# Silu out of the bank on ScalarE, and the norm weight in the product with the gates

## What is computed

```python
def _layer(x, ...):
    proj = x @ w_in                                  # hq hf hi hg rq rk rv rg su
    k_hg, log_f = ...                                # from sigmoid(hf)
    o_hg, s_hg = _chunked_gated_linear(silu(hq), k_hg, hi, log_f, s_hg)
    o_hg = o_hg * rsqrt(mean(o_hg ** 2) + EPS)
    o_hg = o_hg * hg_norm_w * silu(hg)
    o_rt, s_rt = _chunked_gated_linear(rotary(rq), rotary(rk), rv, log_gamma, s_rt)
    o_rt = (o_rt - mean) * rsqrt(var + EPS) * ret_norm_w
    o_rt = o_rt * silu(rg)
    y5 = gelu(s5_scan(su)); y5 = y5 * sigmoid(y5 @ glu_w + glu_b)
    x = layer_norm(ALPHA * x + concat(o_hg, o_rt, y5) @ w_out)
    return layer_norm(ALPHA * x + relu(x @ w_up) ** 2 @ w_down)
```

## Time and profile before

| | us |
|---|---|
| median of 3 runs | 898.17 |
| the profiled execution | 898.88 |
| its span | 897.1 |
| TensorE busy in matmuls | 780.9 |
| VectorE busy | 566.1 |
| ScalarE busy | 381.1 |
| GpSimd busy | 34.9 |

### The profile page before, as it was taken

The page is one execution under the profiler, slowest core; times in us unless marked ns, Lnnn a source line. Parts: engine busy times, 40 slices in busy tenths (PEclk is TensorE's granted clock), DMA queues, the critical chain, the costliest instruction groups (busy, mean ns, idle before and its releaser), DMA issues. The chain is left out here.

```text
span 897.1 us, 16462 instructions
## 1 busy us (share of the span) xinstructions
PE 780.9 (87%) x6750; PEld 736.6 (82%) x6750; DVE 566.1 (63%) x984; ACT 381.1 (42%) x668; POOL 34.9 (4%) x43
## 2 busy tenths in 40 slices
PE   3779778998979978999997987978897999999994
PEld 3778667788879877999996886777796999999993
DVE  7896895334466699764445787745456665466543
ACT  4453111443365622456336622424435554355433
POOL 4000010210000000000000000102000000000000
PEclk9898886987979999999996998989897999999998
DMA  8442111261425534654651332323151566555631
GB/s 333 127 129 72 48 48 48 79 215 45 144 71 165 164 116 143 189 175 129 183 172 48 95 96 71 110 72 102 48 164 38 175 172 195 179 184 169 189 114 49
DMA packets 30587, 113.58 MB, mean 127 GB/s; under 512 B 3520, under 2 KB 3712, under 8 KB 30000
## 3 DMA queue, kind: packets, MB, share of 16 engines
q1 hardware_dynamic: 27936, 101.83, 37.6%
q0 software_dynamic: 2000, 9.62, 2.9%
q10 hardware_dynamic: 576, 1.08, 0.3%
HBM read 108.33 MB, written 4.18 MB: 125 GB/s over the span
## 5 line engine op out<-in xcount | busy, mean ns | idle before, releaser
L1286 DVE TENSOR_TENSOR w_low<-w_raw,w_high 128x1024 fp32r<-128x1024 f32 x192 | 236.9, 1234 | 210.1 <-ACT w_high L949 208.0
L904 PE MATMUL stream<-a_high,w_high 128*128 128x264 f32 x1024 | 319.9, 312 | 43.2 <-DVE a_low L1291 30.2
L949 ACT ACTIVATE w_high<-w_raw 128x1024 fp32r<-128x1024 f32 x192 | 202.1, 1053 | 291.9 <-PE stream L906 257.0
L905 PE MATMUL stream<-a_low,w_high 128*128 128x264 f32 x1024 | 307.5, 300 | 0.0
L906 PE MATMUL stream<-a_high,w_low 128*128 128x264 f32 x1024 | 306.2, 299 | 0.0
L904 PEld LDWEIGHTS stream<-a_high,w_high 128*128 128x128 f32 x1024 | 210.1, 205 | 56.9 <-issue 22.4
L905 PEld LDWEIGHTS stream<-a_low,w_high 128*128 128x128 f32 x1024 | 211.3, 206 | 0.5
L906 PEld LDWEIGHTS stream<-a_high,w_low 128*128 128x128 f32 x1024 | 209.6, 205 | 0.0
L904 PE MATMUL stream<-h_high,w_high 128*128 128x264 f32 x512 | 149.2, 291 | 11.9 <-DVE w_low L1286 9.8
L905 PE MATMUL stream<-h_low,w_high 128*128 128x264 f32 x512 | 145.2, 284 | 0.0
L906 PE MATMUL stream<-h_high,w_low 128*128 128x264 f32 x512 | 145.1, 283 | 0.0
(11 more groups left out here) (325 smaller groups left out, 770.2 us busy)
## 6 DMA issues: line engine op xcount, KB each, us to landing
w_raw<-in_weights SPq DMA_DIRECT2D x192, 512.0 KB, 3.6
mats<-in_matrices POOLq DMA_DIRECT2D x2, 1024.0 KB, 5.4
S_hg<-in_state_hg POOLq DMA_DIRECT2D x2, 768.0 KB, 6.6
out_hg_s<-S_hg POOLq DMA_DIRECT2D x2, 768.0 KB, 4.5
consts<-in_constants POOLq DMA_DIRECT2D x1, 1484.5 KB, 9.4
X<-in_xT ACTq DMA_DIRECT2D x4, 264.0 KB, 5.9
out_y<-X SPq DMA_DIRECT2D x1, 1056.0 KB, 4.0
S_rt<-in_state_rt POOLq DMA_DIRECT2D x2, 512.0 KB, 8.1
```

The lines of the kernel that those rows point to most:

```text
L904: pe.matmul(bnk[:, 0:T], wh, xh, start=(first and kk == 0), stop=False)
L905: pe.matmul(bnk[:, 0:T], wh, xl, start=False, stop=False)
L949: act.activation(w_high[:, n % SPLIT_SLOTS, :], w_raw[:, n % RAW_SLOTS, :], ACT.Copy).then_inc(high_ready, 1)
L1286: put(tt(w_low[:, n % SPLIT_SLOTS, :], w_raw[:, n % RAW_SLOTS, :], w_high[:, n % SPLIT_SLOTS, :].bitcast(F32), ALU.subtract), low_ready)
```

## The change

Silu takes the place of Sigmoid for the queries and the gates, out of the same bank, and ScalarE frees these banks. VectorE's two kinds of products with the banks go. The wide products of `MIX` with the gates become three each, with the norm weight of the feature as a column scale.

```diff
@@ -291,7 +291,6 @@
         y5_done, y5_free = sem("y5_done"), sem("y5_free")
         u_ready = sem("u_ready")
         sig_ready = sem("sig_ready")
-        qsig_ready = sem("qsig_ready")
         gsig_ready = sem("gsig_ready")
         v_ready = sem("v_ready")
         rqk_ready = sem("rqk_ready")
@@ -635,7 +634,7 @@
                     return
                 if r == 0:
                     pe.wait_ge(first_ready, 2 * l + 1)
-                    pe.wait_ge(q_ready, l + 1)
+                    pe.wait_ge(q_ready, 3 * l + 3)
                 pe.wait_ge(dec_ready, 9 * l + r + 1)
                 banks = [unit(l, ("hg_level", r, p)) for p in range(3)]
 
@@ -991,8 +990,9 @@
                     copied(near_top_ready, 9 * l + done, fu)
 
             def gate_sigmoid(l, i):
-                p, _ = tile(l, HGT + i)
-                act.activation(gates[:, i, :], p, ACT.Sigmoid).then_inc(gsig_ready, 1)
+                p, fr = tile(l, HGT + i)
+                act.activation(gates[:, i, :], p, ACT.Silu).then_inc(gsig_ready, 1)
+                copied(gsig_ready, 6 * l + i + 1, fr)
 
             def mixer_work(l, c):
 
@@ -1011,7 +1011,8 @@
                 elif HQ < c <= HQ + 3:
                     i = c - 1 - HQ
                     p, fr = tile(l, HQ + i)
-                    act.activation(Qg[:, i, :], p, ACT.Sigmoid).then_inc(qsig_ready, 1)
+                    act.activation(Qg[:, i, :], p, ACT.Silu).then_inc(q_ready, 1)
+                    copied(q_ready, 3 * l + i + 1, fr)
                 elif SU < c <= SU + 2:
                     i = c - 1 - SU
                     p, fr = tile(l, SU + i)
@@ -1437,12 +1438,6 @@
                 put(tt(s5_end[:, 0, js, :], p1[:, 0, :, :], p3[:, 1, :, :], ALU.subtract))
                 put(tt(s5_end[:, 1, js, :], p1[:, 1, :, :], p3[:, 0, :, :], ALU.add), s5end_ready)
 
-            def hgrn_q(l, j):
-                dve.wait_ge(qsig_ready, 3 * l + j + 1)
-                p, fr = tile(l, HQ + j)
-                put(tt(Qg[:, j, :], Qg[:, j, :], p, ALU.mult), None if j < 2 else q_ready)
-                free(fr)
-
             def s5_sample_inputs(l):
 
                 dve.wait_ge(u_ready, 2 * l + 2)
@@ -1549,13 +1544,12 @@
                 chain(tt(sw, sw, cv("sin").unsqueeze(1).broadcast_to([128, 2, T]), ALU.mult))
                 put(tt(X_[:, :, :], X_[:, :, :], sw, ALU.add), ret_ready)
 
-            def output_gate(l, i):
-
-                dve.wait_ge(gsig_ready, 6 * l + i + 1)
-                p, fr = tile(l, HGT + i)
-                w = pv(l, "hg_norm")[:, 0:1] if i < 3 else pv(l, "ret_norm")[:, i - 3:i - 2]
-                put(stt(gates[:, i, :], gates[:, i, :], w, p, ALU.mult, ALU.mult))
-                free(fr)
+            def output_gate(l, w):
+
+                dve.wait_ge(gsig_ready, 6 * l + 3 * w + 3)
+                for i in range(3 * w, 3 * w + 3):
+                    scale = pv(l, "hg_norm")[:, 0:1] if i < 3 else pv(l, "ret_norm")[:, i - 3:i - 2]
+                    put(stt(MIX[:, i, :], MIX[:, i, :], scale, gates[:, i, :], ALU.mult, ALU.mult))
 
             def hgrn_sample_decay(l):
                 dve.wait_ge(states_loaded, 32 * (l + 1))
@@ -1618,8 +1612,6 @@
                 if c in (S5_FROM[l] + 2, S5_FROM[l] + 3):
                     s5_half(l, c - S5_FROM[l] - 2)
                 s = LATER[l]
-                if 6 <= c < 9:
-                    hgrn_q(l, c - 6)
                 if c == (15, 6)[l]:
                     s5_states(l)
                 if c == (16, 8)[l]:
@@ -1631,6 +1623,8 @@
                     hgrn_sample_add(l, c - 14 - s)
                 if c == (12, 4)[l]:
                     s5_sample_inputs(l)
+                if c == 8 + s:
+                    dve.wait_ge(q_ready, 3 * l + 3)
                 if c == 7 + s:
                     dve.wait_ge(cleared, 4 + l)
                 if 7 + s <= c < 15 + s:
@@ -1662,8 +1656,6 @@
                 if 17 <= c < 20:
                     for h in range(2):
                         ret_scores(l, 2 * (c - 17) + h)
-                if 19 <= c < 24:
-                    output_gate(l, c - 19)
                 if c == 21:
                     for i in range(2):
                         ret_sample_add(l, i)
@@ -1677,17 +1669,16 @@
                         free(fu)
                 if c == (23, 22)[l]:
                     settle()
-                    put(tt(MIX[:, 0:3, :], MIX[:, 0:3, :], gates[:, 0:3, :], ALU.mult))
+                    output_gate(l, 0)
                     head_scale(l, "hg_rs", 0, hmix_ready)
 
             def mixer_end(l):
 
                 for k in range(5):
                     split_a(l, 1, k, MIX, MIX_ORDER[k])
-                output_gate(l, 5)
                 dve.wait_ge(rsq_ready, 3 * l + 3)
                 settle()
-                put(tt(MIX[:, 3:6, :], MIX[:, 3:6, :], gates[:, 3:6, :], ALU.mult))
+                output_gate(l, 1)
                 head_inverse(l, 1, rsd_ready, rrs_ready)
                 head_scale(l, "ret_rs", 1, rmix_ready)
                 for k in range(5, KT):
```

## The result

The changed kernel takes 900.81 us in the median (894.55 to 904.24) against 897.03 us (892.83 to 898.81) for the kernel before, measured beside it: a ratio of 1.0042 [1.0025, 1.0058], slower. The forecast was 897.1 us and, with 0.55, faster. It was wrong in the sign, and the median lies just past the end of its range.

A forecast was written before the change was run, and what follows sets the result against it. TensorE was taken as the bound, so VectorE or ScalarE edits count only through its waits. 898.88 - 7.3 savings + 4.0 bare loads + 2.2 lost clock = 897.8, or 897.1 us beside the median; range 890.3 to 900.8.

The forecast's parts named there:

- The waits at step 19: TensorE's waits for ScalarE's copies near 161 and 606 us, lengthened by bare table loads to 3.2 and 2.6 us.
- I count 1.5 us for the first stall (the size of rows 10) and half of it for the second: Lost clock behind the stalls near 161 and 606 us, sized by an earlier dip at 201 to 206: 2.2 us.
- the bound of 3.0 us for the two falls: Upper limit for clock lost behind the stalls near 161 and 606 us, beside 4.0 us for loads.
- The savings: Shorter TensorE waits for VectorE in both layers, plus clock kept after 201 us: 2.4 + 1.9 + 1.1 + 1.5 + 0.4 = 7.3 us.
- Layer 1's queries: Three query products leave VectorE, the bound from 501 to 549 us, shortening TensorE's wait at 544.99: 1.9 us.
- Step 23: Layer 0 near 199 us: gate product gone ahead of the mean subtraction, 1.1 us, and full clock after, 1.5 more.
- The column 118 to 121: Layer 1's gate product removed ahead of the wait at 639.58 frees 0.63 us, limited by chunk 23's end to 0.4 us.
- the first HGRN level: Layer 0: TensorE starts these scores at about 64.25 instead of 66.63 us, a gain of 2.4 us.
- rival (B): Stalls of step 19 in both layers and the gap near 64 us drop the clock longer: 901.8 us, chance 0.11.
- The six other loads: Added table loads not standing bare at step 19: hidden under other waits, but for some 0.1 us at step 20.
- the prediction's sum by that figure: Three bare loads priced with the page's drain, 2.66 us a switch: 4.1 us more, 901.2 us; given no chance.

The follow-up runs named there:

- d3: Changed kernel with 20 transposes that nobody reads where TensorE stands idle after chunk 19, layer 0 only: 894.23 us, ratio 0.9990 to the kernel before.
- a1: The changed kernel once more, unaltered: 899.20 us, ratio 1.0023 to the kernel before.
- a4: Changed kernel with each layer's first gate moved to the end of step 19, behind the copies TensorE waits for; 19 loads: 888.00 us, ratio 0.9916.
- b3: Changed kernel with Sigmoid for Silu (no added loads, other output) and each layer's first gate at the end of step 19: 886.31 us, ratio 0.9885.
- d2: Repeat of b3: changed kernel with Sigmoid for Silu and the first gate at the end of step 19: 886.63 us, ratio 0.9910.
- c4: Repeat of a4: changed kernel with the first gate at the end of step 19, Silu kept: 887.92 us, ratio 0.9913.
- b2: Only the gates' half of the change, queries as in the kernel before; 17 loads: 901.78 us, ratio 1.0054.
- a3: Kernel before with Silu for Sigmoid at both lines, VectorE's products kept: all loads, no savings, other output: 905.84 us, ratio 1.0114.
- c3: Kernel before with its first gate's sigmoid at the end of step 19 and its product at step 20, no Silu: 897.00 us, ratio 1.0006.
- b1: Only the queries' half of the change, gates as in the kernel before; 17 loads: 892.81 us, ratio 0.9964.
- a2: Changed kernel with Sigmoid for Silu at both lines, so without the eight added loads (other output): 891.96 us, ratio 0.9959.
- d1: Repeat of a2: changed kernel with Sigmoid for Silu at both lines: 891.44 us, ratio 0.9950.
- c1: Changed kernel with the first gate at the end of step 19 in layer 0 only: 892.11 us, ratio 0.9953.

## Why the prediction was wrong, step by step

**The mechanism was right, its size was not.** Eight loads came, at the places named, at 1283 ns each. The waits at step 19 became 3.0 and 2.94 us (predicted 3.2 and 2.6). The waits for VectorE shrank at each place named, the 12 gate products at 489 ns (484 taken) stayed covered, and VectorE's busy time fell by 7.0 us (6.5). The Trainium skill's page ScalarE: Activation LUTs, section "Table sets: the hidden batching unit", had spoken against the change, and its warning held here; but 19 loads beside 13 go with 1.3 to 1.7 us in the median, and it was the place of two in layer 0 and one in layer 1 that cost the rest.

**The step that failed is "I count 1.5 us for the first stall (the size of rows 10) and half of it for the second".** In layer 0 the difference moved by 7.1 us, of which the wait explains 2.4 (3.0 - 0.63); the other 4.7 us I put down to the clock. In layer 1 it moved by 3.2, of which the wait is 1.66 (2.94 - 1.28) and the rest 1.5. So the clock cost 6.2 us and not 2.2.

The stretches bear it out by the prediction's own arithmetic, the missing share of the clock times the length: 0.24 x 7 + 0.35 x 5 + 0.27 x 4 = 4.5 us in layer 0 and 0.27 x 6 = 1.6 in layer 1. The price of one fall of about 3 us was not the mistake: it is 1.5 us by the earlier trace rows, the fall behind the nearer wait of 3.16 us at 544.99 comes to 1.7 (0.59 over 545 to 547 us and 0.55 over 547 to 549 in the kernel before), and layer 1 measured the same. The mistake was to count one such fall in layer 0 and half of one in layer 1. The runs showed a whole one in layer 1 and, in layer 0, one of about 7 us and a second of about 3; falls of about 7 us were in the trace of the kernel before, one of them at a wait that the prediction names (0.57 over 149 to 157 us, and 0.55 over 67 to 72 behind the wait of 2.03 us at 66.63). Even the bound of 3.0 us for the two falls was too low.

That the clock is the cause in layer 0 is shown by d3, which keeps the loads and loses 2.9. In medians, the order of step 19 is worth 11.2 us in the changed kernel (a1 against a4), where 6.1 were forecast for its loads and clock (3.9 and 2.2).

**The savings.** With step 19 out of the way they were 9.8 to 10.4 us (b3, d2), more than the 7.3 summed. Layer 1's queries brought 3.0, not 1.9: the wait for VectorE shrank by 1.6 us, and the four matmuls behind it took 1.13 us instead of 1.72, so a fall of the clock went with it, which the sum hadn't counted. Step 23 brought 2.2 in layer 0 (1.1 + 1.5 predicted), with the clock at 1.00 as foreseen. The column 118 to 121 holds 1.4 in layer 1, where 0.4 were predicted, but after and a1 give some 1 us of it back by chunk 132. At the first HGRN level the start came at 64.47 (64.25 predicted), but behind 3.40 us of idle time, and the clock was at 0.50 from 67 to 72 us (0.55 in the kernel before). In both kernels it was full until that wait and fell behind it, for about 7 us in before and after, for about 10 in a1 and c4. At chunk 14, 10 us further, the changed kernel was 2.2 us ahead in one profile and 0.6 in the other (0.3 to 2.1 in the others that have its queries). The profiles with the queries of before scatter more widely there (b2 is 3.1 us ahead, a3 and c3 are 1.5 behind), so they don't show this gain. The median of b1 leaves some 0.8 of the 2.4 (3.8 us less the 3.0 of layer 1), near what rival (B) had, but with an interval of 1.3 to 5.0 us around its 3.8.

**The six other loads** were to be hidden but for 0.1 us. By differences to before they go with 10.1 (mean of b3 and d2) less 8.1 (mean of a4 and c4), 2.0 us. The profiles agree that they are hidden where they stand (c4 and d2 keep together past all six); the 2 us come with longer falls of the clock behind 640 us, and whether the loads cause them stays open.

**The sum again.** -10.1 + 2.0 + 11.2 = +3.1 us; a1 measured +3.2 and the first measurement +3.8. (The three terms are differences of the same medians, so that they add up proves nothing.) Of the miss against the forecast -1.1, step 19 makes +5.1, the other loads +1.9 and the savings -2.8. The split depends on which part is taken first. With the first gate left in its place, the savings are 4.0 to 5.0 us (a2, d1) where 7.3 were summed, and the eight loads cost 7.2 to 8.3 (differences to before) where 6.2 were summed; then the larger part of the miss is in the savings. The two accounts differ by the 5 us that the order is worth without any load. Both lead to the clock at and behind step 19, which falls there in d1 without an added load and didn't in the kernel before; how much of the 11.2 us belongs to the loads alone, the medians put only between 6 and 8.

**The rivals.** (B) named the right place and the right sign: 901.8, with 0.11. It asked whether the stalls of step 19 drop the clock for longer, and its only argument against was that the clock is "already down" at 64 us. That says nothing of step 19, and it wasn't so: the kernel before has 1.00 from 63 to 67 us and 0.55 from 67 to 72, a fall of about 7 us behind a wait of only 2.03. In layer 0 the clock behind the short wait of step 19 was 1.00, so it had all of it to lose; that was in the earlier trace rows. Its price was near the measured time in part by luck: it had 3.0 us for two falls, where 6.2 were lost, and 3.4 of savings, where there were more.

**What stays open.** Why a wait longer by 0.23 or 0.5 us lets the clock fall in some executions and not in others (d1 against a2 and d2), why the filler of layer 1 moved the fall rather than took it away, and why a stall is followed by a fall of 3 us in one place and of 7 in another. What each piece of the 10 us saving is worth in the median can't be given to better than about 1 us, since the runs of one kernel spread over 8 us wherever the clock is in play.

## What to carry to other kernels

Before an activation function is exchanged, follow its table loads in the engine's order and ask of each what TensorE waits for behind it: six loads under other waits went with 2 us at most, and taking three out of the way of a copy that TensorE waits for gained 11. Price a new stall of TensorE as the wait and the clock it leaves behind, and size the second by all falls of the clock in the profile, the longest too, each whole; where the clock was full before it, the second term can be twice the first (4.7 us against 2.4 here). If such a load can be put behind the copies by moving one instruction, do that first: the same change then gained 8 us in place of losing 3 to 4.

## What the runs showed of the hardware

- Stalls of 3.0 and 2.94 us were followed by 9 us of unbroken work at 0.65 to 0.73 in layer 0 and by 6 us at 0.73 in layer 1; behind 2.70 us in a3 it was 0.50, which is 1.2 GHz throughout.
- Transposes that nobody reads, put into the stall, kept the clock at 1.00 and gave back 4.2 us (7.1 - 2.9) in layer 0; in layer 1 they gave back 1.5 at step 19, and 4.7 were lost by a fall 12 us behind it.
- The spread of the runs goes with the clock: of the 29 runs of the kernel before beside c1 to c4, the fastest took 890.13 us at a mean granted clock of 0.938 and the slowest 898.96 at 0.928. The changed kernel took 894.55 to 904.24 in twenty. With the gate last and no loads, b3 took 886.20 to 886.44 in four runs, all at 0.932, but d2, the same kernel, 885.27 to 890.74 in six, at 0.934 to 0.927.
- Falls of the clock lasted from about 3 us (behind 545 us in the kernel before) to about 14 us (behind 671 us in c4), and the same wait was followed by a fall in one execution and not in the next: 0.23 + 0.63 us at step 19 of layer 0 by two of 3 us in d1 and by none in a2.
- A load starts ahead of its instruction's wait: in c4 the last one ahead of a Sqrt starts at 627.92, and the Sqrt at 632.26, behind a wait of 3.06 us. Where nothing is waited for, the instruction starts 0.01 to 0.02 us behind the load (153.20 + 1.28 and 154.50 above), in every profile here. The Trainium skill's page ScalarE: Activation LUTs, section "What ACT_TABLE_LOAD costs", has a drain of some 1380 ns beside the load; no run shows one, and the measured rows decide. That the prediction's sum by that figure, 901.2 us, lies nearer to the measured 900.81 than its forecast is chance: what made up the difference was the clock.
